# A PEER gate table built by half groups of two tokens, with single-pass float32 one-hots and a gate split in two

## The chip, the core and the metric

The kernel runs on one core of one Trainium2 chip. The metric is the device time of one execution in microseconds: 2560.13 us, the median of three runs (2558.3 to 2563.12). One more execution was recorded by the hardware profiler. It took 2559.59 us, of which the profile's span covers 2557.8 us. The profile calls the engines PE (TensorE; PEld is its weight loading), DVE (VectorE), ACT (ScalarE), POOL (GpSimd) and SP (SyncE, which issues the transfers).

## The reference

Two network blocks in a row over 256 tokens of width 1024. The first has two layers; each ends in a PEER feed-forward, which is where the change lies. Eight heads pick 16 experts each of 128 x 128 for every token, and the experts' outputs are summed with softmax gates:

```python
v1, i1 = lax.top_k(s1, PEER_TOPK)
v2, i2 = lax.top_k(s2, PEER_TOPK)
cand = v1[..., :, None] + v2[..., None, :]
cidx = i1[..., :, None] * PEER_NKEYS + i2[..., None, :]
top, pos = lax.top_k(cand, PEER_TOPK)
eidx = jnp.take_along_axis(cidx, pos, axis=-1)
gate = jax.nn.softmax(top, axis=-1)
...
act = jax.nn.gelu(jnp.einsum('td,thkd->thk', hc, u), approximate=False)
return jnp.einsum('thk,thkd->td', gc * act, expert_v[ec])
```

The kernel does not gather experts. It computes all 16,384 of them for all tokens and multiplies by a dense table of gates that is zero where a token did not pick the expert. That table, G, has for each token 128 x 128 entries: entry (a, b) is the sum of the gates of those of its 128 picks whose first index is a and whose second is b.

## The kernel before

Each layer of the first block is a chain of program blocks (one per phase, with a barrier between). The block in question selects the experts and builds G. Its order in time, in each layer:

1. The query products and key scores; VectorE finds the top 16 of each and combines them. Meanwhile TensorE runs ahead: `ahead()` is a generator that computes the first products of the first 22 pairs of experts, one step (one plain float32 product of 128 x 128 weights with 256 columns, L1204) at a time, 352 steps in all. Half of them (11 pairs) lie before the table, 8 steps follow, and the other 168 are dealt out between the groups of the table by `ahead_by`.
2. The first indices, second indices and gates of all tokens are transposed on TensorE and copied by ScalarE to the tile J (L1288), so that the 128 picks of a token lie on 128 partitions.
3. The table, in 64 groups of 4 tokens (L1223, L1309, L1370, L1292). For each group VectorE compares J with a row of 0..127 and so makes 4 one-hot matrices for the first and 4 for the second indices in one instruction of 1024 columns. GpSimd multiplies the second ones by the gates, in place (512 columns). TensorE makes for each token one plain float32 product of the two (128 contraction rows, 128 columns), four to a PSUM bank. ScalarE copies the bank to G. The one-hots live in 3 of the 4 slots of 1024 columns of the tile one_hots, which lies over ring_hi (the high halves of the weight stream, not used in this phase); VectorE reuses a slot when TensorE has finished the group three earlier (`g_made`). PSUM banks 0 to 3 take the groups in turn.
4. After the last groups ScalarE makes the high halves of the first three weight units of the next block (`split_high`, L345, one after each of the last three groups) and VectorE their low halves (`split_low`, L350). Then comes the barrier. In the next block TensorE waits for VectorE and ScalarE to weight and split the first activations (L1560, L1490, L1572) before L333 starts.

The order on each engine is the order of the code; nothing is rearranged. [...] Plain float32 products appear in the trace as two matrix records with two weight loads each, float32r products as one.

## Time and profile before

| What | Value |
|---|---|
| median of 3 runs | 2560.13 us (2558.3 to 2563.12) |
| the profiled execution | 2559.59 us, span 2557.8 us |
| PE, PEld busy | 94%, 87% of the span |
| DVE, ACT, POOL busy | 68%, 43%, 9% |
| VectorE's one-hots, L1370 | 128 instructions, 185.4 us, mean 1466 ns |
| GpSimd's gates, L1309 | 128 instructions, 228.1 us, mean 1812 ns |
| gate products, L1228 | 1024 matrix records, 135.4 us |
| ScalarE's copies to G, L1292 | 128 instructions, 76.5 us, mean 597 ns |

How to read it: durations of matrix records overlap, since the array is pipelined, so the cost of a product is the distance from its start to the start of the next, and not its duration. The time of a table is read as a stretch: from the first gate product of a layer to the end of TensorE's last run-ahead product. "Idle before" in square brackets names who ended an engine's wait.

### The profile page before, as it was taken

Reading aid. Unit: us, or ns where it says so; the run is one execution under the profiler, and the core shown is the slowest. Engines: PE = TensorE matmul, PEld = TensorE weight load, DVE = VectorE, ACT = ScalarE, POOL = GpSimd, SP = SyncE. Lnnn points to the kernel's source line nnn. Section 1 sums busy time; section 2 is a strip of 40 time slices with the busy share of each in tenths; the row PEclk is TensorE's granted clock in tenths of the full one; section 3 lists DMA queues with packets and bytes.
Section 4 is the critical chain, followed back from the end, with each engine's and each line's share of the span. In section 5 each row is a group of like instructions: output and inputs, shape, how many; then the busy total and the mean of one; then the engine's idle time right before and its main releaser. Section 6 shows DMA issues by size and latency. Waiting matters only on the chain. (4 is left out here: it accounts for less than half of the span.)

```text
span 2557.8 us, 38374 instructions
## 1 busy us (share of the span) xinstructions
PE 2416.8 (94%) x15268; PEld 2214.5 (87%) x15268; DVE 1747.9 (68%) x2811; ACT 1093.5 (43%) x1588; POOL 237.5 (9%) x141
## 2 busy tenths in 40 slices
PE   4889999999999999999999999999999997798998
PEld 4889898889999999899898889999999786788998
DVE  7889876676666666769976675555555677545665
ACT  4541233444444444553133444444444332443554
POOL 0000485000000000000187000000000000000000
PEclk9989999999999999999999999999999898899999
DMA  8455534786666666335533685555555421342553
GB/s 343 146 215 168 157 104 133 272 291 229 238 237 226 234 237 206 118 108 169 179 104 121 223 302 189 188 184 186 188 189 186 146 95 50 116 165 71 194 190 108
DMA packets 133037, 460.58 MB, mean 180 GB/s; under 512 B 15152, under 2 KB 15408, under 8 KB 132400
## 3 DMA queue, kind: packets, MB, share of 16 engines
q1 hardware_dynamic: 132912, 458.90, 52.8%
q8 instruction: 80, 1.31, 0.2%
q14 instruction: 45, 0.37, 0.0%
HBM read 445.73 MB, written 13.11 MB: 179 GB/s over the span
## 5 line engine op out<-in xcount | busy, mean ns | idle before, releaser
L1551 DVE TENSOR_TENSOR ring_lo<-ring,ring_hi 128x1024 fp32r<-128x1024 f32 x421 | 515.3, 1226 | 309.9 <-ACT ring_hi L1485 309.9
L1485 ACT ACTIVATE ring_hi<-ring 128x1024 fp32r<-128x1024 f32 x421 | 445.4, 1058 | 395.5 <-PE banks L335 241.6
L308 PE MATMUL banks<-normed_hi,ring_hi 128*128 128x256 f32 x2096 | 597.8, 285 | 8.9 <-DVE ring_lo L350 8.5
L310 PE MATMUL banks<-normed_hi,ring_lo 128*128 128x256 f32 x2096 | 594.2, 284 | 0.0
L309 PE MATMUL banks<-normed_lo,ring_hi 128*128 128x256 f32 x2096 | 594.2, 283 | 0.0
L308 PEld LDWEIGHTS banks<-normed_hi,ring_hi 128*128 128x128 f32 x2096 | 403.2, 192 | 14.3 <-ACT arena L2248 8.7
L333 PE MATMUL banks<-ring_hi,work_lo 128*128 128x512 f32 x1024 | 401.9, 393 | 11.0 <-DVE work_lo L1572 11.0
L309 PEld LDWEIGHTS banks<-normed_lo,ring_hi 128*128 128x128 f32 x2096 | 403.2, 192 | 3.5
L310 PEld LDWEIGHTS banks<-normed_hi,ring_lo 128*128 128x128 f32 x2096 | 403.0, 192 | 0.0
L334 PE MATMUL banks<-ring_lo,work_lo 128*128 128x512 f32 x1024 | 401.3, 392 | 0.0
L335 PE MATMUL banks<-ring_hi,work_lo 128*128 128x512 f32 x1024 | 400.0, 391 | 0.0
L1204 PE MATMUL banks<-work,ring 128*128 128x256 f32 x1408 | 325.8, 379 | 0.0
L350 DVE TENSOR_TENSOR ring_lo<-ring,ring_hi 128x1024 fp32r<-128x1024 f32 x185 | 224.9, 1223 | 107.4 <-ACT ring_hi L345 107.0
L1204 PEld LDWEIGHTS banks<-work,ring 128*128 128x128 f32 x1408 | 257.4, 190 | 29.5
L1309 POOL TENSOR_TENSOR one_hots<-one_hots,routes 128x512 f32<-128x512 f32 x128 | 228.1, 1812 | 516.9 <-DVE one_hots L1370 516.9
L333 PEld LDWEIGHTS banks<-ring_hi,work_lo 128*128 128x128 f32 x1024 | 193.8, 189 | 50.0 <-DVE work_lo L1572 11.8
L1370 DVE TENSOR_TENSOR one_hots<-routes,consts_sb 128x1024 f32<-128x1024 f32 x128 | 185.4, 1466 | 73.2 <-PE banks L1228 69.3
L345 ACT ACTIVATE ring_hi<-ring 128x1024 fp32r<-128x1024 f32 x185 | 194.9, 1055 | 91.1 <-PE banks L310 57.2
L335 PEld LDWEIGHTS banks<-ring_hi,work_lo 128*128 128x128 f32 x1024 | 193.5, 189 | 41.1
L334 PEld LDWEIGHTS banks<-ring_lo,work_lo 128*128 128x128 f32 x1024 | 193.9, 189 | 37.1
L1292 ACT ACTIVATE arena<-banks 128x512 f32<-128x512 f32 x128 | 76.5, 597 | 169.6 <-PE banks L1228 169.6
L1228 PEld LDWEIGHTS banks<-one_hots 128*128 128x128 f32 x1024 | 134.0, 191 | 8.9 <-POOL one_hots L1309 2.3
(359 smaller groups left out, 3009.4 us busy)
## 6 DMA issues: line engine op xcount, KB each, us to landing
...
```

The lines of the kernel that those rows point to most:

```text
L308: pe.matmul(dst, w_hi[:, o], hi[:, k, :], start=(k == 0), stop=False)
L309: pe.matmul(dst, w_hi[:, o], lo[:, k, :], start=False, stop=False)
L310: mm = pe.matmul(dst, w_lo[:, o], hi[:, k, :], start=False, stop=(k == KD - 1))
L333: pe.matmul(dst, hi[:, t], w_hi[:, o], start=first, stop=False)
L334: pe.matmul(dst, hi[:, t], w_lo[:, o], start=False, stop=False)
L335: mm = pe.matmul(dst, lo[:, t], w_hi[:, o], start=False, stop=last)
L345: act.mark(act.eng.activation(RING_HI[:, u % HIGHS, :], RING[:, u % SLOTS, :], ACT.Copy), "high")
L350: v.mark(v.eng.tensor_tensor(RING_LO[:, u % SLOTS, :], RING[:, u % SLOTS, :], RING_HI[:, u % HIGHS, :].bitcast(F32), ALU.subtract), "split")
L1204: mm = pe.matmul(PS[:, 6 + p % 2, e * T:(e + 1) * T], RING[:, u % SLOTS, k * P:(k + 1) * P], H32[:, k, :], start=(k == 0), stop=(k == KD - 1))
L1309: pool.tensor_tensor(hots[g % HOTS][:, 1], hots[g % HOTS][:, 1], J[:, 2, 4 * g:4 * g + 4].unsqueeze(2).to_broadcast([P, 4, P]), ALU.mult). ...
L1485: sc.activation(RING_HI[:, u % HIGHS, :], RING[:, u % SLOTS, :], ACT.Copy)\
L1551: dve.tensor_tensor(RING_LO[:, u % SLOTS, :], RING[:, u % SLOTS, :], RING_HI[:, u % HIGHS, :].bitcast(F32), ALU.subtract).then_inc(S("spli ...
```

## The change

The table is built in 128 half groups of 2 tokens instead of 64 groups of 4. A slot of 1024 columns now holds four float32r matrices for each of two tokens: the first one-hots, the plain second one-hots, those times the gates' high half, and those times the gates' low half. VectorE makes the first two in one instruction of 512 columns (one-hots are exact in float32r), with the row 0..127 read from PSUM bank 5, where it is copied first. GpSimd makes the high product (256 columns) of every half group; the low product (256 columns) is made by VectorE for even half groups and by GpSimd for odd ones. TensorE accumulates two float32r products per token in place of one plain float32 product. ScalarE makes the rounded gates (GATE_HIGH) with one more copy and VectorE the rest (GATE_LOW) with one subtraction. The run-ahead steps are dealt out over half groups, and ScalarE's three `split_high` come after the half groups whose slots they take, which puts one after group 62 and two after group 63.

```diff
--- before.py
+++ after.py
@@ -1131,15 +1131,19 @@
             PICK = a(3, T)
             G = AR[:, :].rearrange("p (i t) -> p i t", i=P)
             HOTS, GROUPS = HIGHS - 1, T // 4
+            HALVES = 2 * GROUPS
             V0 = 2 * AHEAD
             slot_of = [(S_EXP + V0 + q) % HIGHS for q in range(HIGHS)]
-            hots = [HOT[:, slot_of[(q - GROUPS) % HOTS], :].rearrange("p (m t i) -> p m t i", m=2, t=4) for q in range(HOTS)]
+            slots = [slot_of[(q - HALVES) % HOTS] for q in range(HOTS)]
+            hots_r = [RING_HI[:, q, :].rearrange("p (m t i) -> p m t i", m=4, t=2) for q in slots]
+            GATE_LOW, GATE_HIGH = RS[:, 2, :], RING_HI[:, slots[0], 0:T]
+            IOTA_BANK = PS[:, 5, 0:P]
             STAGE = HOT[:, slot_of[HIGHS - 1], :].rearrange("p (s c) -> p s c", s=2)
             kept = 16 * (AHEAD // 2) * layer
 
             def ahead_by(g):
 
-                return KD + KD * (2 * (AHEAD - AHEAD_PICK) - 1) * (g + 1) // GROUPS
+                return KD + KD * (2 * (AHEAD - AHEAD_PICK) - 1) * (g + 1) // HALVES
 
             with nc.Block() as block:
                 @block.sync
@@ -1220,14 +1224,20 @@
 
                     for _ in range(KD):
                         next(first)
-                    for g in range(GROUPS):
+                    for g in range(HALVES):
+                        if g % 2 == 0:
+                            pe.wait_ge(S("low_gated"), g // 2 + 1)
                         pe.wait_ge(S("gated"), g + 1)
-                        if g >= 4:
-                            pe.wait_ge(S("g_copied"), g - 3)
-                        for t in range(4):
-                            mm = pe.matmul(PS[:, g % 4, t * P:(t + 1) * P], hots[g % HOTS][:, 0, t, :],
-                                           hots[g % HOTS][:, 1, t, :], start=True, stop=True)
-                        mm.then_inc(S("g_made"), 1)
+                        if g >= 8 and g % 2 == 0:
+                            pe.wait_ge(S("g_copied"), g // 2 - 3)
+                        for t in range(2):
+                            o = (2 * (g % 2) + t) * P
+                            dst = PS[:, g // 2 % 4, o:o + P]
+                            pe.matmul(dst, hots_r[g % HOTS][:, 0, t, :], hots_r[g % HOTS][:, 2, t, :],
+                                      start=True, stop=False)
+                            mm = pe.matmul(dst, hots_r[g % HOTS][:, 0, t, :], hots_r[g % HOTS][:, 3, t, :],
+                                           start=False, stop=True)
+                        mm.then_inc(S("half_made"), 1)
                         for _ in range(ahead_by(g) - (ahead_by(g - 1) if g else KD)):
                             next(first)
                     for _ in first:
@@ -1285,17 +1295,21 @@
                     by_tile(2, GT.rearrange("p a b -> p (a b)"))
                     for i in range(3):
                         act.wait("routes_turned", i + 1)
-                        act.mark(sc.activation(J[:, i, :], PS[:, nxt(), 0:T], ACT.Copy), "bank_emptied")
+                        b = nxt()
+                        if i == 2:
+                            act.mark(sc.activation(GATE_HIGH, PS[:, b, 0:T], ACT.Copy), "gate_high")
+                        act.mark(sc.activation(J[:, i, :], PS[:, b, 0:T], ACT.Copy), "bank_emptied")
                     p = AHEAD_PICK
                     for g in range(GROUPS):
-                        act.wait("g_made", g + 1)
+                        act.wait("half_made", 2 * g + 2)
                         act.mark(sc.activation(G[:, :, 4 * g:4 * g + 4],
                                                PS[:, g % 4, :].rearrange("p (t i) -> p i t", t=4), ACT.Copy), "g_copied")
-                        if ahead_by(g) >= 2 * KD * (p + 1 - AHEAD_PICK):
+                        if ahead_by(2 * g + 1) >= 2 * KD * (p + 1 - AHEAD_PICK):
                             ahead_gelu(p)
                             p += 1
-                        if g >= GROUPS - PRE:
-                            split_high(act, S_EXP + V0 + g - (GROUPS - PRE), True)
+                        for q in range(PRE):
+                            if (HALVES - PRE + q) // 2 == g:
+                                split_high(act, S_EXP + V0 + q, True)
                     while p < AHEAD:
                         ahead_gelu(p)
                         p += 1
@@ -1304,11 +1318,17 @@
 
                 @block.gpsimd
                 def _(pool):
-                    for g in range(GROUPS):
+                    pool.wait_ge(S("gate_low"), 1)
+                    for g in range(HALVES):
                         pool.wait_ge(S("one_hots"), g + 1)
-                        pool.tensor_tensor(hots[g % HOTS][:, 1], hots[g % HOTS][:, 1],
-                                           J[:, 2, 4 * g:4 * g + 4].unsqueeze(2).to_broadcast([P, 4, P]),
-                                           ALU.mult).then_inc(S("gated"), 1)
+                        plain = hots_r[g % HOTS][:, 1].bitcast(F32)
+                        i = pool.tensor_tensor(hots_r[g % HOTS][:, 2], plain,
+                                               J[:, 2, 2 * g:2 * g + 2].unsqueeze(2).to_broadcast([P, 2, P]), ALU.mult)
+                        if g % 2:
+                            i = pool.tensor_tensor(hots_r[g % HOTS][:, 3], plain,
+                                                   GATE_LOW[:, 2 * g:2 * g + 2].unsqueeze(2).to_broadcast([P, 2, P]),
+                                                   ALU.mult)
+                        i.then_inc(S("gated"), 1)
 
                 @block.vector
                 def _(dve):
@@ -1363,14 +1383,22 @@
                     v(dve.reciprocal(GS, GS), "gate")
                     v(dve.tensor_tensor(GT, GT, GS.unsqueeze(2).to_broadcast([P, 16, 16]), ALU.mult), "routed")
 
+                    v.wait("q_copied", N_WQ)
+                    v(dve.tensor_copy(IOTA_BANK, iota), "iota_banked")
                     v.wait("bank_emptied", 3)
-                    for g in range(GROUPS):
+                    v(dve.tensor_tensor(GATE_LOW, J[:, 2, :], GATE_HIGH.bitcast(F32), ALU.subtract), "gate_low")
+                    for g in range(HALVES):
                         if g >= HOTS:
-                            v.wait("g_made", g - HOTS + 1)
-                        v.mark(dve.tensor_tensor(hots[g % HOTS], J[:, 0:2, 4 * g:4 * g + 4].unsqueeze(3)
-                                                 .to_broadcast([P, 2, 4, P]),
-                                                 iota.unsqueeze(1).unsqueeze(1).to_broadcast([P, 2, 4, P]),
+                            v.wait("half_made", g - HOTS + 1)
+                        v.mark(dve.tensor_tensor(hots_r[g % HOTS][:, 0:2], J[:, 0:2, 2 * g:2 * g + 2].unsqueeze(3)
+                                                 .to_broadcast([P, 2, 2, P]),
+                                                 IOTA_BANK.unsqueeze(1).unsqueeze(1).to_broadcast([P, 2, 2, P]),
                                                  ALU.is_equal), "one_hots")
+                        if g % 2 == 0:
+                            v.wait("one_hots", g + 1)
+                            v.mark(dve.tensor_tensor(hots_r[g % HOTS][:, 3], hots_r[g % HOTS][:, 1].bitcast(F32),
+                                                     GATE_LOW[:, 2 * g:2 * g + 2].unsqueeze(2).to_broadcast([P, 2, P]),
+                                                     ALU.mult), "low_gated")
                     highs = N_WQ - PRE
                     for q in range(PRE):
                         split_low(v, S_EXP + V0 + q, highs + q)
```

On PE, at the start of the table in the first layer, before (L1204 is the run-ahead product; stage0_11 is raised by GpSimd's gates, stage0_13 by ScalarE's copy):

```order
L1228 MATMUL banks<-one_hots 128x128 [waits stage0_11]
L1228 MATMUL banks<-one_hots 128x128 x3
L1204 MATMUL banks<-work,ring 128x256 [waits loaded5]
L1204 MATMUL banks<-work,ring 128x256
L1228 MATMUL banks<-one_hots 128x128 [waits stage0_11]
L1228 MATMUL banks<-one_hots 128x128 x3
L1204 MATMUL banks<-work,ring 128x256 x3
```

The same place after the change (L1208 is the run-ahead product; stage0_12 is raised by GpSimd, stage0_11 by VectorE's low gates):

```order
L1236 MATMUL banks<-ring_hi 128x128 [waits stage0_12,stage0_11]
L1238 MATMUL banks<-ring_hi 128x128
L1236 MATMUL banks<-ring_hi 128x128
L1238 MATMUL banks<-ring_hi 128x128
L1208 MATMUL banks<-work,ring 128x256 [waits loaded5]
L1236 MATMUL banks<-ring_hi 128x128 [waits stage0_12]
L1238 MATMUL banks<-ring_hi 128x128
L1236 MATMUL banks<-ring_hi 128x128
L1238 MATMUL banks<-ring_hi 128x128
L1208 MATMUL banks<-work,ring 128x256
```

Four products of one kind between run-ahead steps have become two blocks of four of the other kind, each with waits of its own.

On DVE at the start of the table, before (stage0_12 is TensorE's report that a group is made):

```order
L1364 TENSOR_TENSOR arena<-arena 128x256 [waits stage0_24]
L1370 TENSOR_TENSOR one_hots<-routes,consts_sb 128x1024 [waits stage0_20,stage0_19]
L1370 TENSOR_TENSOR one_hots<-routes,consts_sb 128x1024 x2
L1370 TENSOR_TENSOR one_hots<-routes,consts_sb 128x1024 [waits stage0_12] x61
L350 TENSOR_TENSOR ring_lo<-ring,ring_hi 128x1024 [waits stage0_16] x3
```

And after (L1399 is the low gates of an even half group; stage0_24 is VectorE's own report that the one-hots are written, stage0_13 TensorE's that a half group is made):

```order
L1384 TENSOR_TENSOR arena<-arena 128x256 [waits stage0_27]
L1387 COPY banks<-consts_sb 128x128 [waits stage0_6,stage0_20]
L1389 TENSOR_TENSOR rstd<-routes,ring_hi 128x256 [waits stage0_21,stage0_28]
L1393 TENSOR_TENSOR ring_hi<-routes,banks 128x512 [waits stage0_23]
L1399 TENSOR_TENSOR ring_hi<-ring_hi,rstd 128x256 [waits stage0_24]
L1393 TENSOR_TENSOR ring_hi<-routes,banks 128x512 x2
L1399 TENSOR_TENSOR ring_hi<-ring_hi,rstd 128x256 [waits stage0_24]
L1393 TENSOR_TENSOR ring_hi<-routes,banks 128x512 [waits stage0_13] x2
```

VectorE's one long instruction per four tokens has become three short ones, of which the low gates have two operands in SBUF.

On ACT at the end of the table, before (L1292 copies a group to G, L1267 is the last activation of the run-ahead products, L345 a high half of a weight unit):

```order
L1292 ACTIVATE arena<-banks 128x128x4 [waits stage0_12] x4
L345 ACTIVATE ring_hi<-ring 128x1024 [waits loaded2]
L1292 ACTIVATE arena<-banks 128x128x4 [waits stage0_12]
L345 ACTIVATE ring_hi<-ring 128x1024 [waits loaded3]
L1292 ACTIVATE arena<-banks 128x128x4 [waits stage0_12]
L1267 ACTIVATE one_hots<-banks 128x512 [waits spilled1,units_used]
L345 ACTIVATE ring_hi<-ring 128x1024 [waits loaded4]
```

And after:

```order
L1305 ACTIVATE arena<-banks 128x128x4 [waits stage0_13] x5
L345 ACTIVATE ring_hi<-ring 128x1024 [waits loaded2]
L1305 ACTIVATE arena<-banks 128x128x4 [waits stage0_13]
L1277 ACTIVATE one_hots<-banks 128x512 [waits spilled1,units_used]
L345 ACTIVATE ring_hi<-ring 128x1024 [waits loaded3]
L345 ACTIVATE ring_hi<-ring 128x1024 [waits loaded4]
```

The second high half has moved behind the last activation, which waits for TensorE's last run-ahead product.

## Rows read from the trace of the kernel before

**Rows 1.** Busy time by window, the table of each layer: us and instructions per engine.

```profile
295.78:425.98 130.20, 130.20 (x848) 120.79 (x848) 91.87 (x64) 45.66 (x76) 112.03 (x63) 1.00 0.35 110
1273.00:1403.00 130.00, 130.00 (x848) 120.73 (x848) 91.80 (x64) 45.66 (x76) 111.97 (x63) 1.00 0.35 110
```

**Rows 2.** Timeline in the table: start us, us, engine, line, count, idle before.

```profile
352.43 1.08 PEld L1228 LDWEIGHTS banks<-one_hots 128*128 128x128 f32 x8
...
353.43 1.17 PEld L1204 LDWEIGHTS banks<-work,ring 128*128 128x128 f32 x6
...
354.62 1.08 PEld L1228 LDWEIGHTS banks<-one_hots 128*128 128x128 f32 x8
...
355.62 0.73 PEld L1204 LDWEIGHTS banks<-work,ring 128*128 128x128 f32 x4
...
356.38 1.08 PEld L1228 LDWEIGHTS banks<-one_hots 128*128 128x128 f32 x8
```

**Rows 3.** Source view of the one-hots L1370: what VectorE waited for, us, times.

```profile
  PE banks L1228: 69.3, 98
```

**Rows 4.** Timeline of POOL and DVE, where both want to run.

```profile
295.69 2.02 POOL L1309 TENSOR_TENSOR one_hots<-one_hots,routes 128x512 f32<-128x512 f32 x1
...
296.98 1.81 DVE L1370 TENSOR_TENSOR one_hots<-routes,consts_sb 128x1024 f32<-128x1024 f32 x1 [0.17 <-PE banks L1228]
...
297.67 2.02 POOL L1309 TENSOR_TENSOR one_hots<-one_hots,routes 128x512 f32<-128x512 f32 x1
...
355.84 1.04 POOL L1309 TENSOR_TENSOR one_hots<-one_hots,routes 128x512 f32<-128x512 f32 x1
...
```

**Rows 5.** Source views of weight loads, shortest/median/longest ns: plain, float32r, transposes.

```profile
L1732 PEld LDWEIGHTS banks<-arena,normed x32: 190/192/338, 2024.9 to 2029.1; 128*128 128x128 f32 x32
...
L308 PEld LDWEIGHTS banks<-normed_hi,ring_hi x2096: 186/192/337, 51.2 to 2538.7; 128*128 128x128 f32 x191
...
L2221 PEld LDWEIGHTS banks<-consts_sb,arena x16: 137/140/143, 2307.8 to 2310.9; 128*128 128x128 f32 x16
```

**Rows 6.** Timeline of PE: plain products of 12 columns; float32r ones of 256 and 512.

```profile
2025.14 1.40 PE L1732 MATMUL banks<-arena,normed 128*128 128x12 f32 x12
...
699.91 0.28 PE L309 MATMUL banks<-normed_lo,ring_hi 128*128 128x256 f32 x1
700.03 0.28 PE L310 MATMUL banks<-normed_hi,ring_lo 128*128 128x256 f32 x1
700.15 0.40 PE L333 MATMUL banks<-ring_hi,work_lo 128*128 128x512 f32 x1
700.38 0.40 PE L334 MATMUL banks<-ring_lo,work_lo 128*128 128x512 f32 x1
```

**Rows 7.** Source views of VectorE: 512 columns from PSUM and SBUF; 256 columns.

```profile
L975 DVE TENSOR_TENSOR arena<-banks,arena x16: 680/682/692, 69.8 to 1083.2; 128x512 f32<-128x512 f32 x16
...
L2414 DVE TENSOR_TENSOR part_at<-arena,part_at x22: 418/419/425, 2369.0 to 2542.9; 128x256 fp32r<-128x256 f32 x22
```

**Rows 8.** Timeline, start of the table.

```profile
291.36 1.01 ACT L1288 ACTIVATE routes<-banks 128x256 f32<-128x256 f32 x3
...
292.47 4.34 DVE L1370 TENSOR_TENSOR one_hots<-routes,consts_sb 128x1024 f32<-128x1024 f32 x3 [1.98 <-ACT routes L1288]
...
295.78 1.16 PE L1228 MATMUL banks<-one_hots 128*128 128x128 f32 x8 [0.38 <-POOL one_hots L1309]
```

**Rows 9.** Timeline, end of the table and start of the next block.

```profile
426.02 0.60 ACT L1267 ACTIVATE one_hots<-banks 128x512 f32<-128x512 f32 x1 [0.70 <-PE banks L1204]
...
426.51 1.05 ACT L345 ACTIVATE ring_hi<-ring 128x1024 fp32r<-128x1024 f32 x1
427.59 1.23 DVE L350 TENSOR_TENSOR ring_lo<-ring,ring_hi 128x1024 fp32r<-128x1024 f32 x1 [2.26 <-ACT ring_hi L345]
...
429.36 0.69 DVE L1560 TENSOR_TENSOR work<-rstd,arena 128x512 f32<-128x512 f32 x1 [0.54 <-DVE ring_lo L350]
...
431.49 0.80 PE L333 MATMUL banks<-ring_hi,work_lo 128*128 128x512 f32 x1 [5.51 <-DVE work_lo L1572]
```

## The prediction

> **What bounds the kernel now.** I read the stretches of the table first, since the change touches nothing else but its two ends. In each layer TensorE is busy for all of the 130.2 us and GpSimd for 112 of them, at full granted clock [rows 1]: the reader is to see that TensorE has no hole, and that GpSimd is not far behind. The timeline then splits TensorE's time. A group with three run-ahead steps lasts 2.19 us from weight load to weight load, one with two steps 1.76 [rows 2]. So a step costs 0.43 us, and a group's four gate products, eight records, 0.90, which is 0.111 a record. With 168 steps, 2.625 a group, a group takes 0.90 + 1.13 = 2.03 us. VectorE waits for TensorE 98 times [rows 3], so the one-hots are ahead.
>
> The next view is of the two engines that feed TensorE. An undisturbed gate instruction on GpSimd lasts 1.04 us, most take 2.02 [rows 4]. Each engine is held until the other is done: VectorE's instruction of 296.98 ends at 298.79, 1.08 us after GpSimd's end at 297.71, and GpSimd's of 297.67 ends at 299.69, 0.90 after that. The reader is to see two instructions in turn, 1.98 us a pair, just below TensorE's 2.03. The Trainium skill states this as an exclusive lock (SBUF — State Buffer, "Who interferes with whom"): VectorE with two SBUF operands and a GpSimd instruction that reads SBUF block each other; the trace agrees with its 1.08 and 0.90.
>
> **The change, part by part, for one group of four tokens.**
>
> TensorE: eight plain records go, eight float32r records of 128 columns come. No row shows that form. At 256 columns float32r products start 0.12 us apart, at 512 columns 0.23 [rows 6], about 0.11 for 256 more columns: 128 columns alone would be some 0.07. But plain products of 12 columns also start 0.10 to 0.11 apart (12 records in 1.40, the last lasting 0.26) [rows 6], so there the weight load is what costs. A float32r weight load lasts 192 ns like the plain one, while the transposes' lasts 140 [rows 5]; I take it that the float32r load costs as much as the plain one. Bounds: 0.067 and 0.12 a record; I take 0.111, from the nearest load, which makes a group 8 x 0.111 + 1.13 = 2.02. The load of a block's first record can lie beside the run-ahead product ahead of it, which may save up to 0.09 in each of the two blocks (1.86). With 0.067 it is 8 x 0.067 + 1.13 = 1.67, with 0.12 it is 2.09.
>
> VectorE: one instruction of 1.08 to 1.22 goes; two of 512 columns with one PSUM operand come at 0.685 [rows 7], back to back some 0.08 less, as the starts in rows 4 overlap ends, and one of 256 columns at 0.42 [rows 7] after a wait of 0.03 for its own one-hots. Sum 2 x 0.605 + 0.45 = 1.66: below TensorE. Only the 256-column one has two SBUF operands; at a quarter of the 1.08 us that 1024 columns hold the port [rows 4], it holds GpSimd off for some 0.28.
>
> GpSimd: one instruction of 512 columns goes, three of 256 come. From 0.14 of start (1.04 - 0.90) and 0.90 for 512 columns, of which I leave 0.05 fixed, one of 256 takes 0.61 alone and 0.57 in a row; bounds 0.52 (half of 1.04) and 0.70. Three in a row are 1.72, and 0.28 for VectorE's, less the 0.10 of a start that hides behind it, make 1.90.
>
> So each engine alone stays below 2.03. Together they needn't. When an even half group's one-hots are ready, VectorE's low gates ask for the port while GpSimd is in the odd half group before. If they get it only after GpSimd's last instruction, this runs in series: low gates 0.28, next one-hots 0.605, signal 0.08, GpSimd's high 0.61 and low 0.57: 2.15 us per group, longer than TensorE needs. If they slip in between GpSimd's two, the group costs GpSimd's 1.90 or TensorE's own time. The slots make this tighter: three hold one and a half groups now, where they held three, so VectorE can't run ahead over such a wait. I take 2.08, the middle between TensorE's 2.02 and the chain's 2.15: 64 x 2.08 = 133.1 us against 130.2, +2.9 a layer. The ends of this case are 2.04 (+0.4) and 2.15 (+7.4).
>
> The head of the table: TensorE waited 0.38 for the first gates [rows 8]. Now ScalarE makes one more copy (1.01 for three [rows 8], 0.34), VectorE the low gates' table (0.45), then one-hots 0.69, signal 0.08, GpSimd 0.61 and 0.28 of being held: from 292.47 ready at 294.9, before TensorE is free at 295.4. The wait goes: -0.4. The copy of the row 0..127 to PSUM lies in VectorE's idle 1.98 [rows 8] and costs nothing; without that cover it would be 0.3.
>
> The tail: of the three high halves, one was behind ScalarE's last activation, now two are, as the order on ACT shows. That activation waits for TensorE's end; VectorE's low half follows (426.51 + 1.05, then 1.23), and the next block's first VectorE instruction and TensorE's first product wait for it, TensorE standing idle for 5.51 [rows 9]. A second low half starts at 428.74 instead of ending at 428.82: it ends at 429.97, +1.15 on the path, and nothing covers it.
>
> Sum over two layers: 2 x (2.9 - 0.4 + 1.15) = +7.3 us. The profiled execution of 2559.59 us (span 2557.8) would come to 2566.9; it stands 0.54 below the median of the runs, so the median forecast is 2567.4, said as 2567. What this measurement can tell from no change is about 0.2%, 5 us.
>
> **The rivals.**
>
> First, faster: TensorE's float32r product is cheap (0.067, or most loads hide) and VectorE's low gates always slip in, so that GpSimd's 1.90 sets the pace. For it: GpSimd's two odd instructions leave a gap, and float32r at 512 columns streams one column per 2.4 GHz cycle [rows 6]. Against it: the weight loads of rows 5, and the even step's timing. Time: 64 x 1.90 = 121.6, -8.6, with the ends -7.9 a layer: 2544. The Trainium skill counts a true float32 product as four passes (FP8 and Floating Point Precision, "TensorE Precision Notes"), which would make two single-pass ones half as dear; at half of 0.90 TensorE's group would be 1.58, and GpSimd's 1.90 would still hold the time at 2544. Rows 2 and 6 agree with four against one at equal columns (0.43 against 0.12 at 256), not at 128 yet.
>
> Second, no change: TensorE stays the bound at 2.02, the feeders keep up. Time: only the ends remain, 2 x 0.75: 2562. For it: all three sums are below 2.03. Against it: the series of 2.15.
>
> Third, much slower: GpSimd's small instructions carry a larger fixed part. At 0.70 and 0.66 in a row the series is 2.33, +19 a layer, 2600; if VectorE's PSUM operand doesn't free the port, the port's holds are 2 x 0.55 + 0.28 + 3 x 0.47 = 2.79, +49 a layer: 2660. Rows 4 can't exclude either. By the skill's rule (same section) an instruction of VectorE with one SBUF operand doesn't contend; no run here shows it yet.
>
> Fourth: a float32r product of 128 columns costs more than the plain one, say 0.216: 8 x 0.216 + 1.13 = 2.86, +53 a layer: 2667. Rows 6 speak against it, being at one column per cycle.
>
> **How the numbers follow.** The series in some groups (forecast) 0.50, the first rival 0.27, the second 0.12, the third 0.07, the fourth 0.04. The forecast's own range is 2562 to 2576 (2.04 to 2.15); its lowest tenth is within 0.2%. The whole range reaches down to the first rival, 2544, less the 1 us of scatter, and up to half of the third's lower price, 2590. Slower: 0.45 + 0.11 = 0.56; same: 0.12 and that tenth, 0.17; faster: the first rival, 0.27.
>
> **What would show it.** In the profile after: the float32r records 0.11 apart (0.07 is the first rival); GpSimd's 256-column instructions at 0.61 or 0.9, never 2.0; VectorE's one-hots at 0.69 whatever GpSimd does, its low gates 0.42 or, held, 0.7 to 1.0; TensorE waiting some 0.05 us a group for VectorE's or GpSimd's gates; each table 133 us; the gap before L333's counterpart 6.7 instead of 5.5. The prediction is wrong if TensorE doesn't wait in the table, or if GpSimd is busy without a break there.

## The result: 2569.5 us against 2560.1, and the profile after

The changed kernel takes 2569.51 us, the median of 7 runs (2566.39 to 2571.18), against 2560.13 for the kernel before (7 runs, 2557.73 to 2563.45): a ratio of 1.0035, 95% interval 1.0024 to 1.0047. That interval is 6.1 to 12.0 us more. The forecast was 2567, +7.3. The profiled execution has a span of 2567.0 us, 9.2 more than before, with a mean granted clock of 0.973 against 0.972.

In the view of busy time by window (columns: length; PE, PEld, DVE, ACT and POOL busy with their instructions; granted clock, DMA share, GB/s) the two tables of the changed kernel are (each window opens 0.11 us ahead of its first gate product; the lengths are those of the tables):

```profile
292.66:427.78 135.12, 134.87 (x851) 118.82 (x849) 119.24 (x191) 44.18 (x75) 123.90 (x191) 1.00 0.34 106
1275.13:1410.26 135.13, 134.88 (x851) 118.80 (x849) 119.28 (x191) 44.19 (x75) 123.92 (x191) 1.00 0.35 106
```

The reader is to see a table of 135.1 us where [rows 1] had 130.2: +4.92 in each layer. (The second window of [rows 1] is 130.00 long; read from first gate product to last run-ahead product that table takes 130.20 too.) VectorE is busy for 119 us of it instead of 92 and GpSimd for 124 instead of 112, and neither for all of it. PE's 134.87 is close to full only because the modelled records overlap the waits; PEld, busy for 118.8 of 135.1 us where it was busy for 120.8 of 130.2, shows the holes better. The source views name who ended the waits (idle time in us, and how many times, over both layers). The first line is what the gate products L1236 waited for, the second what the one-hots L1393 waited for; then come the lengths (shortest/median/longest ns) of VectorE's low gates and of GpSimd's high and low ones:

```profile
  POOL ring_hi L1328: 17.1, 50
```

```profile
  PE banks L1238: 21.2, 64
```

```profile
L1399 DVE TENSOR_TENSOR ring_hi<-ring_hi,rstd x128: 424/520/858, 291.6 to 1406.1; 128x256 fp32r<-128x256 f32 x128
...
L1325 POOL TENSOR_TENSOR ring_hi<-ring_hi,routes x256: 605/613/797, 291.8 to 1407.6; 128x256 fp32r<-128x256 f32 x128
...
L1328 POOL TENSOR_TENSOR ring_hi<-ring_hi,rstd x128: 605/612/891, 293.3 to 1408.1; 128x256 fp32r<-128x256 f32 x128
```

TensorE now waits for GpSimd's low gates, 17.1 us in 50 places; before, it waited for GpSimd 3.0 us in 6 places. Nearly all of the 17.1 is idle time of the weight load, part of which lies beside a product that still runs, so 8.5 us a layer lengthen a table by less. VectorE waits for TensorE for 21.2 us instead of the 69.3 of [rows 3]. GpSimd's instructions of 2.02 us [rows 4] are gone. What is left of the two engines' turns at the port is in the timeline of POOL and DVE (start, length, engine, line; in brackets the idle time before, and who ended it):

```profile
352.42 0.47 DVE L1399 TENSOR_TENSOR ring_hi<-ring_hi,rstd 128x256 fp32r<-128x256 f32 x1
352.56 0.79 POOL L1325 TENSOR_TENSOR ring_hi<-ring_hi,routes 128x256 fp32r<-128x256 f32 x1
...
352.81 1.33 DVE L1393 TENSOR_TENSOR ring_hi<-routes,banks 128x512 fp32r<-128x512 f32 x2
...
353.56 0.61 POOL L1325 TENSOR_TENSOR ring_hi<-ring_hi,routes 128x256 fp32r<-128x256 f32 x1 [0.20 <-DVE ring_hi L1393]
...
354.13 0.61 POOL L1328 TENSOR_TENSOR ring_hi<-ring_hi,rstd 128x256 fp32r<-128x256 f32 x1
...
354.17 0.85 DVE L1399 TENSOR_TENSOR ring_hi<-ring_hi,rstd 128x256 fp32r<-128x256 f32 x1
...
354.70 0.79 POOL L1325 TENSOR_TENSOR ring_hi<-ring_hi,routes 128x256 fp32r<-128x256 f32 x1
```

Read it as a ring. VectorE's low gates stand ready at 354.17, 0.04 after GpSimd has begun its own low gates (354.13). They get through when GpSimd is done, at 354.70, and hold up its next instruction, 0.79 instead of 0.61. The next one-hots stand behind them on VectorE. One turn earlier, at 352.56, the same happened, and shows what follows: GpSimd, done with the even half at 353.35, sits idle for 0.20 until the odd half's one-hots are written (353.56). From 352.56 to 354.70 it is 2.14 us for a group, where TensorE needs 2.02.

Not every group runs so. Ten microseconds earlier VectorE's low gates come 0.02 ahead of GpSimd's:

```profile
343.73 0.42 DVE L1399 TENSOR_TENSOR ring_hi<-ring_hi,rstd 128x256 fp32r<-128x256 f32 x1
343.75 0.88 POOL L1328 TENSOR_TENSOR ring_hi<-ring_hi,rstd 128x256 fp32r<-128x256 f32 x1
...
344.59 1.18 POOL L1325 TENSOR_TENSOR ring_hi<-ring_hi,routes 128x256 fp32r<-128x256 f32 x2
...
346.30 0.79 POOL L1325 TENSOR_TENSOR ring_hi<-ring_hi,routes 128x256 fp32r<-128x256 f32 x1
```

Now GpSimd is the one that is held, for 0.88, and its group, begun at 342.18, lasts 2.41 us. The next one, from 344.59 to 346.30, has no hold in it and lasts 1.71. The pair is 4.12 us, 2.06 a group. Counted over each table by the starts of GpSimd's even half groups, 31 groups of 63 last 2.14 us, 16 last 2.41 and 16 last 1.71, in a pattern that comes again every eight groups. Together that is 2.10 a group. In all 32 groups of 2.41 us of the two tables VectorE's low gates start 0.00 to 0.02 ahead of GpSimd's, and in all others 0.04 to 0.42 behind: who is first at the port, by a few hundredths of a microsecond, goes with which of the two patterns runs.

TensorE's own records of the new kind (float32r, printed as fp32r where it is written: the 4-byte operands that take one matrix record a product where plain float32 takes two) start 0.11 us apart within a block; the first of a block stands 0.25 ahead, beside the run-ahead product before it:

```profile
350.91 0.41 PE L1236 MATMUL banks<-ring_hi 128*128 128x128 f32 x1
...
351.16 0.27 PE L1238 MATMUL banks<-ring_hi 128*128 128x128 f32 x1
...
351.27 0.27 PE L1236 MATMUL banks<-ring_hi 128*128 128x128 f32 x1
...
351.38 0.28 PE L1238 MATMUL banks<-ring_hi 128*128 128x128 f32 x1
```

The head of the table has lost its wait of 0.38 [rows 8], but the second half group has one of 0.25:

```profile
292.77 0.41 PE L1236 MATMUL banks<-ring_hi 128*128 128x128 f32 x1
...
294.24 0.33 PE L1236 MATMUL banks<-ring_hi 128*128 128x128 f32 x1 [0.25 <-POOL ring_hi L1328]
```

The end of the table, to be held against [rows 9]:

```profile
427.93 0.60 ACT L1277 ACTIVATE one_hots<-banks 128x512 f32<-128x512 f32 x1 [0.32 <-PE banks L1208]
428.42 1.99 ACT L345 ACTIVATE ring_hi<-ring 128x1024 fp32r<-128x1024 f32 x2
429.50 2.36 DVE L350 TENSOR_TENSOR ring_lo<-ring,ring_hi 128x1024 fp32r<-128x1024 f32 x2 [1.64 <-ACT ring_hi L345]
432.40 0.69 DVE L1588 TENSOR_TENSOR work<-rstd,arena 128x512 f32<-128x512 f32 x1 [0.54 <-DVE ring_lo L350]
...
434.53 0.79 PE L333 MATMUL banks<-ring_hi,work_lo 128*128 128x512 f32 x1 [6.64 <-DVE work_lo L1600]
```

Two high halves stand behind the last activation, two low halves behind them, and TensorE stands idle for 6.64 us instead of 5.51. Per layer that makes 4.92 + 1.13 - 0.38 = 5.67, and 11.3 for two. Measured are 9.4 (medians) and 9.2 (spans). The rest lies outside these stretches: the first table starts 2.6 us earlier than the 0.38 explains, the way from its end to the second table takes 0.4 less, and what follows the second table 0.9 more. No change of the code explains these three. The first gate product starts anywhere from 292.8 to 298.8 us in the traces of this study, and 11.3 lies inside the interval of the runs, so 2 us of a single execution need no cause of their own.

### The profile page after: what moved, and what is told of

The parts are those of the page before. It is cut to its first block and busy times, and to the rows that moved or that the text cites. A ratio compares the mean times of both kernels' runs of the same rounds, so it can differ in the third digit from the quotient of the medians.

```text
span 2567.0 us, 38904 instructions
## 1 busy us (share of the span) xinstructions
PE 2421.4 (94%) x15268; PEld 2208.7 (86%) x15268; DVE 1802.5 (70%) x3071; ACT 1092.6 (43%) x1590; POOL 258.8 (10%) x397
## 5 line engine op out<-in xcount | busy, mean ns | idle before, releaser
L333 PE MATMUL banks<-ring_hi,work_lo 128*128 128x512 f32 x1024 | 401.1, 392 | 13.3 <-DVE work_lo L1600 13.3
L1208 PE MATMUL banks<-work,ring 128*128 128x256 f32 x1408 | 359.5, 388 | 0.0
L1208 PEld LDWEIGHTS banks<-work,ring 128*128 128x128 f32 x1408 | 247.7, 191 | 22.9
L333 PEld LDWEIGHTS banks<-ring_hi,work_lo 128*128 128x128 f32 x1024 | 193.4, 189 | 51.9 <-DVE work_lo L1600 14.1
L345 ACT ACTIVATE ring_hi<-ring 128x1024 fp32r<-128x1024 f32 x185 | 194.7, 1054 | 93.2 <-PE banks L310 59.6
L1325 POOL TENSOR_TENSOR ring_hi<-ring_hi,routes 128x256 fp32r<-128x256 f32 x256 | 172.6, 679 | 506.8 <-DVE ring_hi L1393 506.8
L1393 DVE TENSOR_TENSOR ring_hi<-routes,banks 128x512 fp32r<-128x512 f32 x256 | 171.3, 681 | 24.2 <-PE banks L1238 21.2
L1236 PE MATMUL banks<-ring_hi 128*128 128x128 f32 x512 | 157.7, 334 | 0.5 <-POOL ring_hi L1328 0.5
```

The source lines that it names most:

```text
L333: pe.matmul(dst, hi[:, t], w_hi[:, o], start=first, stop=False)
L345: act.mark(act.eng.activation(RING_HI[:, u % HIGHS, :], RING[:, u % SLOTS, :], ACT.Copy), "high")
L1208: mm = pe.matmul(PS[:, 6 + p % 2, e * T:(e + 1) * T], RING[:, u % SLOTS, k * P:(k + 1) * P], H32[:, k, :], start=(k == 0), stop=(k == KD - 1))
L1325: i = pool.tensor_tensor(hots_r[g % HOTS][:, 2], plain, J[:, 2, 2 * g:2 * g + 2].unsqueeze(2).to_broadcast([P, 2, P]), ALU.mult)
```

## The experiments

Twelve kernels were run. "Table" is the stretch from the first gate product to TensorE's last run-ahead product, "gap" TensorE's wait before L333; both layers agree within 0.03 us in every kernel, and 0.1 us of a table is more than its scatter (experiments 1 and 5, which have the same table, differ by 0.01). The kernel before, timed beside them, took 2559.77 us (experiments 1 to 4), 2559.49 (5 to 8), 2558.67 (9 and 10) and 2560.05 (11 and 12). Experiments 2, 3, 4, 7, 8, 10 and 11 were timed once. Executions of one kernel spread over some 6 us, so where times are that close the tables and gaps carry the argument.

| Kernel | us | table | gap |
|---|---|---|---|
| before | 2560.13 | 130.20 | 5.51 |
| after | 2569.51 | 135.12 | 6.64 |
| 1 low gates read from PSUM | 2561.64 | 131.13 | 6.65 |
| 2 high product only | 2562.78 | 132.33 | 6.64 |
| 3 row 0..127 from SBUF | 2660.77 | 179.02 | 6.65 |
| 4 two slots | 2648.46 | 173.16 | 7.78 |
| 5 as 1, high halves earlier | 2560.09 | 131.12 | 5.73 |
| 6 groups of 4, one fp32r product | 2502.69 | 101.46 | 5.51 |
| 7 low gates after the odd one-hots | 2562.89 | 131.86 | 6.64 |
| 8 all low gates on GpSimd | 2591.43 | 146.62 | 6.64 |
| 9 groups of 4, two bfloat16 halves | 2536.82 | 118.68 | 5.51 |
| 10 half groups alone | 2573.17 | 135.06 | 6.64 |
| 11 half groups, row from PSUM | 2561.71 | 129.86 | 6.65 |
| 12 as 9, low gates shared | 2511.18 | 105.06 | 5.51 |

**1. Free the port of the low gates.**

```diff
+            LOW_BANK = PS[:, 5, P:P + T]
...
+                        if g == 0:
+                            v(dve.tensor_copy(LOW_BANK, GATE_LOW), "low_banked")
                         if g % 2 == 0:
...
-                                                     GATE_LOW[:, 2 * g:2 * g + 2].unsqueeze(2).to_broadcast([P, 2, P]),
+                                                     LOW_BANK[:, 2 * g:2 * g + 2].unsqueeze(2).to_broadcast([P, 2, P]),
```

> The changed kernel with one edit: VectorE's copy of the low gates lies in PSUM too, so that its low-gate product has one SBUF operand. The changed kernel's table takes 135.1 us a layer (before: 130.2). Series theory (low gates of VectorE and the gates of GpSimd wait for each other at the port, 2.13 us a group): with the port free VectorE needs 1.66, GpSimd 1.72, so TensorE's 2.02 sets the pace, table 130 us, time 2560 (no change against before, since the tail's 2 x 1.13 stays and the head's 0.38 may come back). Rival, the product itself (two float32r products cost TensorE 2.11): table stays 135, 2569. Rival, three slots of half groups are too few: table stays 133 to 135.

Measured: 2561.64 us (11 runs), ratio to before 1.0006 (0.9997 to 1.0015); tables of 131.13. In the source views of the low gates and of GpSimd's high ones nothing is held any more, and TensorE's waits for GpSimd, 17.1 us in the changed kernel, shrink to 4.9 (4.3 at the weight load, in 16 places, and 0.6 at the product):

```profile
L1402 DVE TENSOR_TENSOR ring_hi<-ring_hi,banks x128: 420/420/422, 292.6 to 1399.8; 128x256 fp32r<-128x256 f32 x128
...
L1326 POOL TENSOR_TENSOR ring_hi<-ring_hi,routes x256: 610/614/618, 292.4 to 1400.9; 128x256 fp32r<-128x256 f32 x128
...
  PEld banks L1237: 4.3, 16
```

The same instructions in the same order, with one operand moved from SBUF to PSUM (and one copy more, once a layer), give back 4.0 of the 4.9 us per table. Without the holds at the port there is no loss of that size.

**2. Half of TensorE's gate work left out.** The low gates are made, but their product is left out.

```diff
                             pe.matmul(dst, hots_r[g % HOTS][:, 0, t, :], hots_r[g % HOTS][:, 2, t, :],
-                                      start=True, stop=False)
-                            mm = pe.matmul(dst, hots_r[g % HOTS][:, 0, t, :], hots_r[g % HOTS][:, 3, t, :],
-                                           start=False, stop=True)
+                                      start=True, stop=True)
```

> The changed kernel with TensorE making only the high product of each token; the low gates are still made and waited for, so the table lacks their part. TensorE then needs 4 x 0.11 + 1.13 = 1.58 us a group. Series theory: the table stays at 2.13 a group, 134 to 136 us. Rival, TensorE's products set the pace: 135 - 64 x 0.45 = 106 us, or at least GpSimd's own 1.72 to 1.90, 110 to 122 us.

Measured: 2562.78 us, tables of 132.33. By its own sum TensorE now needs only 4 x 0.111 + 1.13 = 1.57 a group, and it waits for GpSimd in 160 places:

```profile
  POOL ring_hi L1326: 100.6, 160
```

Neither expectation came, the 134 to 136 of the series no more than the 106 or 110 to 122 of the rival. GpSimd's groups here alternate between 2.41 and 1.71 us from the first to the last, and the groups of 2.14 are gone. So 2.07 us a group is the pace of VectorE and GpSimd with TensorE out of the way. It is a little above TensorE's 2.02, so no price of a float32r product could have made the change a gain. But TensorE's work has a part in the loss: with half of it gone, 2.8 of the 4.9 us come back. The loss is what the two feeders and TensorE do to each other's timing, and not the pace of either side alone.

**3. Does the PSUM operand free the port?**

```diff
-                                                 IOTA_BANK.unsqueeze(1).unsqueeze(1).to_broadcast([P, 2, 2, P]),
+                                                 iota.unsqueeze(1).unsqueeze(1).to_broadcast([P, 2, 2, P]),
```

> The changed kernel with VectorE's comparison reading the row 0..127 from SBUF as before, so that all its instructions have two SBUF operands. If two SBUF operands hold the port against GpSimd: 2 x 0.55 + 0.28 + 3 x 0.47 = 2.8 us a group, table 179 us, time 2657; comparisons of 0.69 become up to 1.2. If the PSUM operand frees nothing: table 135, 2569.

Measured: 2660.77 us, tables of 179.02, a group of 2.80 us. The source views of GpSimd's high gates and VectorE's one-hots (613 and 685 ns in the changed kernel) show both held:

```profile
L1325 POOL TENSOR_TENSOR ring_hi<-ring_hi,routes x256: 608/1056/1061, 295.8 to 1500.4; 128x256 fp32r<-128x256 f32 x128
...
L1393 DVE TENSOR_TENSOR ring_hi<-routes,consts_sb x256: 679/956/1104, 294.9 to 1498.8; 128x512 fp32r<-128x512 f32 x128
```

This is the second case of the third rival: its price was 2.79 us a group and 2660 us. In the change itself the operand does free the port. The Trainium skill says (SBUF — State Buffer, "Who interferes with whom") that VectorE with at most one SBUF input does not contend with GpSimd. The traces agree: 613 ns at the median in the changed kernel against 1056 here, and 610 to 618 for all 256 in experiment 1, where no instruction of VectorE has two SBUF operands.

**4. Slots.**

```diff
-            HOTS, GROUPS = HIGHS - 1, T // 4
+            HOTS, GROUPS = HIGHS - 2, T // 4
...
-                            if (HALVES - PRE + q) // 2 == g:
+                            if (HALVES - 1) // 2 == g:
```

> The changed kernel with two slots of half groups in place of three (the three high halves of weights all come after the last group, which adds some 1 us to the tail). Series theory with the slots just deep enough at three: with two, a comparison waits for the half group two earlier, and the loop comparison 0.69, signal 0.08, GpSimd 0.61 or 1.18, TensorE 0.6 runs twice per two slots: 2.0 even, 2.6 odd, so 2.3 to 2.4 a group, table 147 to 154 us. If depth plays no part even here: 135. If three slots are already the bound (2.13 is the slots' loop), the loss is larger, near 3/2 x 2.13: 200 us.

Measured: 2648.46 us, tables of 173.16 (2.71 us a group). VectorE waits for TensorE at 250 of the 256 one-hots, and TensorE for GpSimd's low gates in 222 places. VectorE's waits:

```profile
  PE banks L1238: 99.5, 250
```

(The gap is longer because all three high halves now come after the last half group.) With two half groups in flight VectorE cannot start one before TensorE is done with the one before the last. It cost more than the 147 to 154 us of the series theory and less than the 200 of three slots as the bound: two slots are too few. Whether a fourth would help the changed kernel was not run.

**5. The tail.** Experiment 1 with the high halves ahead of the last activation; the edit against experiment 1:

```diff
-                        if ahead_by(2 * g + 1) >= 2 * KD * (p + 1 - AHEAD_PICK):
-                            ahead_gelu(p)
-                            p += 1
                         for q in range(PRE):
                             if (HALVES - PRE + q) // 2 == g:
                                 split_high(act, S_EXP + V0 + q, True)
+                        if ahead_by(2 * g + 1) >= 2 * KD * (p + 1 - AHEAD_PICK):
+                            ahead_gelu(p)
+                            p += 1
```

> This is the kernel of the first experiment (VectorE's low gates read from PSUM) with ScalarE's high halves of the next block's first three weight units placed ahead of the last activation of the run-ahead products instead of around it. If the longer gap after the table comes from the high half that stands behind that activation, the gap before L333's counterpart falls from 6.65 us to at most the 5.5 of before, the tables stay at 131.1, and the time is 2561.6 - 2 x 1.1 = 2559.4, the same as before. If the gap is set by something else in the next block, it stays at 6.6 and the time at 2561.6. If the activation, pushed back by the copies in front of it, becomes the late one, the gap lies in between.

Measured: 2560.09 us (11 runs), ratio to before 1.0003 (0.9994 to 1.0012). The timeline of the first layer's end:

```profile
425.02 1.99 ACT L345 ACTIVATE ring_hi<-ring 128x1024 fp32r<-128x1024 f32 x2
426.11 2.36 DVE L350 TENSOR_TENSOR ring_lo<-ring,ring_hi 128x1024 fp32r<-128x1024 f32 x2 [0.53 <-ACT ring_hi L345]
426.92 0.59 ACT L1278 ACTIVATE one_hots<-banks 128x512 f32<-128x512 f32 x1
...
431.14 0.79 PE L333 MATMUL banks<-ring_hi,work_lo 128*128 128x512 f32 x1 [5.73 <-DVE work_lo L1603]
```

The gap falls from 6.65 to 5.73. The order on ScalarE makes most of the longer gap, as predicted. Of the fall to 5.5 that was expected 0.22 is missing, which fits the last two high halves: they still start only after the last half group's products. The whole time does not tell experiments 1 and 5 apart; the gap does.

**6. What a float32r product costs with enough feeding.** From the kernel before; the low half of the gates is left out.

```diff
-            hots = [HOT[:, slot_of[(q - GROUPS) % HOTS], :].rearrange("p (m t i) -> p m t i", m=2, t=4) for q in range(HOTS)]
+            hots = [RING_HI[:, slot_of[(q - GROUPS) % HOTS], :].rearrange("p (m t i) -> p m t i", m=2, t=4) for q in range(HOTS)]
+            IOTA_BANK = PS[:, 5, 0:P]
...
+                    v(dve.tensor_copy(IOTA_BANK, iota), "iota_banked")
...
-                                                 iota.unsqueeze(1).unsqueeze(1).to_broadcast([P, 2, 4, P]),
+                                                 IOTA_BANK.unsqueeze(1).unsqueeze(1).to_broadcast([P, 2, 4, P]),
```

> The kernel before, in groups of four, with the one-hots and the gates written in float32r and one float32r product per token; the row 0..127 comes from PSUM. The low half of the gates is left out. If a float32r product of 128 columns costs 0.111 us like a plain record, a group costs TensorE 4 x 0.111 + 1.13 = 1.57 us, and the feeders (VectorE some 1.1, GpSimd 1.04 without holds) keep up: the table is 64 x 1.57 = 101 us, 29 less per layer, and the time 2560 - 58 = 2502. If the table's pace is not TensorE's but that of the engines that feed it, it stays near 130 and the time near 2560. If the product cost 0.067, the table would be 90 and the time 2480.

Measured: 2502.69 us (4 runs), ratio 0.9776 (0.9761 to 0.9791); tables of 101.46, 28.7 less each. By window TensorE is busy throughout, GpSimd for 65 us:

```profile
296.13:397.59 101.46, 101.46 (x595) 92.54 (x593) 77.87 (x64) 45.20 (x76) 65.48 (x63) 1.00 0.45 141
```

101.46 / 64 = 1.585 a group, so (1.585 - 1.13) / 4 = 0.114 a product. At 128 columns a float32r product costs one record and a plain one two records of 0.111, so two products for one is an even trade, here in groups of four tokens and, by experiments 1 and 11 below, in groups of two. The Trainium skill counts four passes for a true float32 product (FP8 and Floating Point Precision, "TensorE Precision Notes"); the ratio here is two.

**7. The ring cut at another place.** VectorE makes the even half's low gates after the odd half's one-hots.

```diff
-                        if g % 2 == 0:
-                            v.wait("one_hots", g + 1)
+                        if g % 2:
+                            e = g - 1
+                            v.wait("one_hots", e + 1)
...
```

> The changed kernel with VectorE's low gates of an even half group placed behind the one-hots of the odd half group that follows, on VectorE alone; same work, same operands. If the loss is the series low gates, next one-hots, signal, GpSimd's high and low (the odd one-hots wait behind low gates that wait for the port), the odd one-hots no longer stand behind the low gates and the table falls from 135.1 to between 131 and 133 us, the time to some 2561 to 2566. If the loss is the port's total occupation, it stays at 135. Against it: TensorE's block for the even half group now waits for low gates that come 0.6 us later, which with three slots could give a wait of its own; then it is 137 or more.

Measured: 2562.89 us, tables of 131.86. The low gates still have both operands in SBUF and still hold GpSimd's high gates (680 ns on the average, 679 in the changed kernel; its low ones take 608 instead of 679), but they no longer wait themselves for long (539 ns at most instead of 858), and no odd half's one-hots stand behind them, and TensorE's waits for both add up to 12.2 us over two layers where they were 17.1 for GpSimd alone:

```profile
  DVE ring_hi L1400: 7.1, 46
  POOL ring_hi L1328: 5.1, 18
```

So the amount of work at the port is not the loss, but the order in which it is asked for and what stands behind the one that waits: 3.3 of the 4.9 us come back with the same instructions in another order.

**8. All low gates on GpSimd.** TensorE then has no wait for VectorE's.

```diff
-                        if g % 2:
+                        if True:
                             i = pool.tensor_tensor(hots_r[g % HOTS][:, 3], plain,
...
-                        if g % 2 == 0:
-                            v.wait("one_hots", g + 1)
-                            v.mark(dve.tensor_tensor(hots_r[g % HOTS][:, 3], hots_r[g % HOTS][:, 1].bitcast(F32),
...
```

> The changed kernel with all low gates made by GpSimd, none by VectorE. VectorE then never takes the port. If GpSimd's instructions are what they are when alone (0.61 the first and 0.57 the second of a pair), it needs 4 x 0.57 = 2.3 us per group, is the bound, and the table is 64 x 2.3 = 147 us (time some 2593). If it were the port's conflicts and not GpSimd's own time that set the pace, the table would fall below 135. If GpSimd waits for one-hots besides, it is over 150.

Measured: 2591.43 us, tables of 146.62, 2.29 us a group; by window GpSimd is busy for 145.0 us of it:

```profile
293.09:439.71 146.62, 146.62 (x849) 113.71 (x848) 87.15 (x126) 44.16 (x75) 145.02 (x254) 1.00 0.32 98
```

Four instructions at 0.573 from start to start are 2.29. GpSimd's term for instructions in a row (0.57) was right.

**9. The same table in bfloat16.** Groups of four; what the gates have beyond two bfloat16 halves is left out.

```diff
+        HOTB = nc.alloc_sbuf_tensor_at("one_hots_b", [P, HIGHS, 2 * D], BF16, offset=-(-nc.sbuf_base // 32) * 32)
...
+            hots = [HOTB[:, q, :].rearrange("p (m t i) -> p m t i", m=4, t=4) for q in slots]
...
+                            pe.matmul(dst, hots[g % HOTS][:, 0, t, :], hots[g % HOTS][:, 2, t, :],
+                                      start=True, stop=False)
+                            mm = pe.matmul(dst, hots[g % HOTS][:, 0, t, :], hots[g % HOTS][:, 3, t, :],
+                                           start=False, stop=True)
...
+                        v.mark(dve.tensor_tensor(hots[g % HOTS][:, 3], hots[g % HOTS][:, 1],
+                                                 LOW_BANK[:, 4 * g:4 * g + 4].unsqueeze(2).to_broadcast([P, 4, P]),
+                                                 ALU.mult), "low_gated")
```

> The kernel before in groups of four, with the one-hots and both halves of the gates in bfloat16 (four matrices of four tokens fill a slot): GpSimd makes the high gates (512 columns), VectorE the low ones (512 columns) from a table in PSUM, TensorE two bfloat16 products per token. What the gates have beyond their two bfloat16 halves is left out. This measures what the gate product costs when operands have 2 bytes. If its 0.111 us is the loading of 4-byte weights, a record of 128 columns falls to between 0.053 (one column per 2.4 GHz cycle) and 0.07, TensorE needs 8 x 0.06 + 1.13 = 1.6 us a group, VectorE becomes the bound with 1.14 + 0.60 = 1.74 and some signal time, and the table is 111 to 118 us: the time some 2522 to 2536. If the record stays at 0.111, the table is TensorE's 2.02 x 64 = 129 to 130 us and the time 2560. GpSimd's 512 columns should stay at 1.04 since VectorE takes one operand from PSUM; if they go to 2.0, bfloat16 changes the lock and the table comes near 130 as well.

Measured: 2536.82 us (4 runs), ratio 0.991 (0.9893 to 0.9926); tables of 118.68. The timeline of PE and its weight loads:

```profile
350.54 0.10 PEld L1235 LDWEIGHTS banks<-one_hots_b 128*128 128x128 bf16 x1
350.59 0.22 PE L1235 MATMUL banks<-one_hots_b 128*128 128x128 bf16 x1
350.60 0.10 PEld L1237 LDWEIGHTS banks<-one_hots_b 128*128 128x128 bf16 x1
350.65 0.22 PE L1237 MATMUL banks<-one_hots_b 128*128 128x128 bf16 x1
```

The products start 0.055 us apart, and the weight load lasts 98 ns instead of 191. The numbers of columns are unchanged; only the operands' type differs, for the weights and for the columns that are multiplied by them. The columns are not what costs 0.11: 256 more of them in float32r cost 0.11 together, and plain products of 12 columns also start 0.10 to 0.11 apart [rows 6]. That leaves the loading of 4-byte weights. The Trainium skill gives the direction (TensorE: Matmul & The Clock Gate, "Weight-path perf modes"): a faster weight load for types other than float32, about twice as fast; the trace agrees, with float32r loading like float32. VectorE's two instructions (1.21 and 0.69) follow each other at 1.85 a group and set the pace.

**10. The halving alone, with plain float32 products.**

```diff
-            hots = [HOT[:, slot_of[(q - GROUPS) % HOTS], :].rearrange("p (m t i) -> p m t i", m=2, t=4) for q in range(HOTS)]
+            hots = [HOT[:, slot_of[(q - HALVES) % HOTS], 0:4 * P].rearrange("p (m t i) -> p m t i", m=2, t=2) for q in range(HOTS)]
...
-                    for g in range(GROUPS):
+                    for g in range(HALVES):
...
```

> The kernel before with half groups of two tokens and nothing else of the change: one-hots of 512 columns from two SBUF operands, gates of 256 columns in place, one plain float32 product per token, ScalarE's high halves in the changed order. It prices the halving alone. If the halving costs nothing in the table, TensorE stays the bound: table 130 to 131 us, gap before L333's counterpart 6.6, time 2560 + 2 x 1.1 = 2562. If the handing over of the port costs more with twice as many instructions (one-hots 0.5 + gates 0.5, twice a group, and four starts of 0.1), the pair takes 2.2 us a group or more, and the table is 140 or more.

Measured: 2573.17 us, tables of 135.06. Neither of the expected cases: the loss is there, at half the size of the second one. GpSimd's gates and VectorE's one-hots, both with two SBUF operands, are held, and TensorE waits:

```profile
L1312 POOL TENSOR_TENSOR one_hots<-one_hots,routes x256: 606/1055/1134, 292.1 to 1409.3; 128x256 f32<-128x256 f32 x128
...
L1373 DVE TENSOR_TENSOR one_hots<-routes,consts_sb x256: 676/767/1102, 291.3 to 1407.9; 128x512 f32<-128x512 f32 x128
...
  PEld banks L1230: 16.6, 46
```

So half groups on the operands of before would have cost as much as the whole change did.

**11. The same with the row 0..127 in PSUM.** The edit against experiment 10:

```diff
+            IOTA_BANK = PS[:, 5, 0:P]
...
+                    v(dve.tensor_copy(IOTA_BANK, iota), "iota_banked")
...
-                                                 iota.unsqueeze(1).unsqueeze(1).to_broadcast([P, 2, 2, P]),
+                                                 IOTA_BANK.unsqueeze(1).unsqueeze(1).to_broadcast([P, 2, 2, P]),
```

> Half groups with one plain float32 product as in the run before, but the row 0..127 comes from PSUM, so that VectorE's one-hots have one SBUF operand. The run before lost 4.9 us per table with the halving alone. If that loss is the two engines taking turns at the port (2.11 us per group for two pairs against 1.98 for the one long pair), GpSimd's instruction falls from 0.97 to 0.61 us and the table to TensorE's 130 to 131 us; the time is 2573 - 2 x 4.5 = 2564 at most, 2562 by the gap alone. If it is the three slots that now hold one and a half groups, the table stays at 135 with GpSimd's instruction at 0.61 and TensorE still waiting.

Measured: 2561.71 us, tables of 129.86. GpSimd's gates last 614 ns, and TensorE has no wait in the table:

```profile
L1313 POOL TENSOR_TENSOR one_hots<-one_hots,routes x256: 612/614/616, 293.5 to 1400.4; 128x256 f32<-128x256 f32 x128
```

Three slots of half groups are therefore no loss by themselves. (The 0.34 less than before stands in the first groups, where the kernel before still waits for GpSimd.) Experiment 1 differs in the two float32r products and the low gates, and takes 131.13 - 129.86 = 1.27 us more. The trace shows that this is not the products' price. In both kernels a group without a wait lasts 2.188 us (three run-ahead steps) or 1.757 (two) on TensorE, and so it does in the kernel before. Of the 1.27, 0.58 are in the first group, where TensorE waits and one more copy stands ahead of the low gates on VectorE, and 0.5 are seven waits of 0.07. The other 0.19 is mostly how a table is read: the first record of a float32r block begins some 0.14 us earlier, beside the run-ahead product.

**12. A version that beats both.** Experiment 9 with two of four low gates on GpSimd, from a copy of their table in SBUF; part of the edit against experiment 9:

```diff
+                        pool.tensor_tensor(hots[g % HOTS][:, 3, 2:4], hots[g % HOTS][:, 1, 2:4],
+                                           LOW_SB[:, 4 * g + 2:4 * g + 4].unsqueeze(2).to_broadcast([P, 2, P]),
+                                           ALU.mult).then_inc(S("gated"), 1)
...
-                        v.mark(dve.tensor_tensor(hots[g % HOTS][:, 3], hots[g % HOTS][:, 1],
-                                                 LOW_BANK[:, 4 * g:4 * g + 4].unsqueeze(2).to_broadcast([P, 4, P]),
+                        v.mark(dve.tensor_tensor(hots[g % HOTS][:, 3, 0:2], hots[g % HOTS][:, 1, 0:2],
+                                                 LOW_BANK[:, 4 * g:4 * g + 2].unsqueeze(2).to_broadcast([P, 2, P]),
```

> The bfloat16 kernel, with two of each group's four low gates (256 columns) moved from VectorE to GpSimd. What the gates have beyond their two bfloat16 halves is left out. VectorE needs 1.24 + 0.35 = 1.6 us a group instead of 1.85, GpSimd 1.04 - 0.05 + 0.57 = 1.56 plus the signal, TensorE 8 x 0.055 + 1.13 = 1.57. If the last kernel was bound by VectorE's two instructions alone, the table falls from 118.7 to between 101 and 106 us, the time to 2537 - 2 x (13 to 17) = 2503 to 2511. If the three engines in a row (one-hots, then gates, then products) leave a wait with three slots, the table is 106 to 115 and the time 2511 to 2530. If GpSimd's second instruction with both operands in SBUF is held back or dearer in bfloat16, the table stays near 118.

Measured: 2511.18 us (4 runs), ratio 0.9795 (0.9746 to 0.9843); tables of 105.06:

```profile
298.67:403.73 105.06, 104.93 (x848) 89.91 (x848) 99.97 (x127) 45.20 (x76) 100.18 (x127) 1.00 0.43 136
```

All three engines are busy for 95% of the table or more. It beats before and after by 49 and 58 us, at the price of gates of two bfloat16 halves. Experiment 6 is faster still, but keeps only the high half.

## Why the prediction was right, and where a size was off

**The likeliest case came, in half of the groups.** The forecast was the series through the port in some groups, and the trace has it: the ring of 2.14 us (forecast 2.15) and its members, low gates behind GpSimd's last instruction, one-hots behind the low gates, GpSimd idle for 0.20. Experiment 1 takes away the holds at the port, experiment 7 only the order, and each takes away most of the loss. Experiment 2 shows that the product's price alone is not it, but also that the ring does not run when TensorE has half its gate work: TensorE's load belongs to the cause. How its timing brings VectorE's low gates 0.04 behind GpSimd's in one group and 0.02 ahead in another was not tested.

**The term that was mis-sized** is the pace of that case. I took 2.08 a group, "the middle between TensorE's 2.02 and the chain's 2.15"; it measured 135.12 / 64 = 2.11, inside the case's own 2.04 to 2.15, and made +4.9 a layer instead of +2.9. The half was right, 31 groups of 63; what failed is the lower end of the middle. Outside the ring a group does not cost TensorE's 2.02. The prediction gave low gates that slip in between GpSimd's two instructions a price of "GpSimd's 1.90 or TensorE's own time". They cost 2.41 and 1.71 in turn, 2.06 a group: the group in which GpSimd's low gates are held also has the 0.20 of idle time. Together that is 2.10, and the rest of the 2.11 stands at the two ends of the table.

**TensorE**: float32r records 0.11 apart, as taken from the weight loads and against the 0.067 that the columns alone gave. Experiment 6 confirms the price, and experiment 9 the reason. The 0.09 that a block's first load might have saved did not come: groups without a wait last 2.19 and 1.76 us as before.

**VectorE and GpSimd**: 0.69, 0.42 and 0.61 as forecast; VectorE's low gates held for up to 0.86 (forecast 0.7 to 1.0), GpSimd at most 0.89 and never 2.0. Experiment 8 confirms 0.57 in a row to 0.003.

**Slots**: three cost nothing where VectorE does not hold GpSimd (experiment 11), and two cost much (experiment 4). That three make the waits at the port worse, as the prediction says, stays open: a fourth slot was not run.

**Head and tail**: -0.38 for -0.4, with 0.25 of it coming back one half group later; +1.13 for +1.15, with experiment 5 for its cause.

**The sum**: 2 x (4.92 - 0.38 + 1.13) = 11.3 for 7.3. The medians show 9.4, since stretches outside the tables gave 2 us back, for which no cause was found. The total is thus closer to the forecast than its main term is, by luck.

**The rivals.** The first needed low gates that always slip in: they do so in every second group at most, and then the pair costs 2.06 a group and not 1.90. Its other condition, a cheap product, would have given back 2.8 us a table and still left it 2.1 above the 130.2 of before (experiment 2). The second, TensorE as the bound, is what experiments 1 and 5 make of the change: 2561.6 and 2560.1. The third's first condition, a larger fixed part on GpSimd, is refuted by 0.61; its second is experiment 3, 2660.8 for 2660. That this agrees to 1 us is in part rounding: 64 x 2.79 is 48.4 us a layer above before and not 49, which makes 2658. The fourth is refuted: 0.114 for the 0.216 it needed.

**The range.** The upper end was to be half of the third's lower price, said as 2590; half of its +40 us would be 2580. Nothing hangs on it here. But a range from 2543 to 2590 has room for a gain and for a loss; what the measurement tests is the forecast's own 2562 to 2576.

**A theory that came late.** Before experiments 10 and 11 I held the halving to be free. It is free only because the change also moved a VectorE operand to PSUM. With twice as many turns at the port the table of experiment 10 takes 2.11 us a group; the one long pair of [rows 4] took 1.98, which TensorE's 2.03 could cover.
